# A seven-product down projection in another order: the bias row joins p1 on VectorE, and its second half reaches the residual by two transfers

## What is computed

```python
hc = conv_b + sum(conv_w[i] * hp[:, i:i + T] for i in range(CONV_WIDTH))
g, u = hc[..., :D_FF], hc[..., D_FF:]
y = jnp.einsum('btf,fd->btd', jax.nn.gelu(g, approximate=False) * u, w_down)   # D_FF = 2816, d = 1024
x = layer_norm(DEEPNORM_ALPHA * x + y, ln2_g, ln2_b)
```

## Time and profile before

| | us |
|---|---|
| time, median of 3 runs | 2312.85 (2310.52 to 2314.06) |
| the profiled execution | 2320.86 |
| its span, first to last instruction | 2319.1 |
| mean granted TensorE clock | 0.975 |
| PE busy | 2156.8 (93%) |
| DVE busy | 1605.3 (69%) |
| ACT busy | 1046.3 (45%) |
| POOL busy | 887.4 (38%) |
| down projection, first layer (first to last matmul on L2718) | from 883.9 |
| the same, second layer | to 2303.6 |
| DMA moved | 338.93 MB, mean 146 GB/s |

### The profile page before, as it was taken

One profiled execution on the slowest core, in us unless ns is written; L12 is line 12 of the kernel. 1 busy time (PEld: TensorE's weight loads), 2 busy tenths in 40 slices (PEclk: granted clock), 3 DMA queues, 4 the chain that ended last, 5 costly groups with the idle time before them and its releaser, 6 DMA issues.

```text
span 2319.1 us, 35307 instructions
## 1 busy us (share of the span) xinstructions
PE 2156.8 (93%) x13868; PEld 1937.6 (84%) x13868; DVE 1605.3 (69%) x2064; ACT 1046.3 (45%) x1867; POOL 887.4 (38%) x554
## 2 busy tenths in 40 slices
PE   7999999899999998789899999989999999988996
PEld 7997677899999997678688866769999999966775
DVE  1477767877777777455845687577777777775467
ACT  3226655444434444344522276464443444353543
POOL 1115255554455452121221342445545544333122
PEclk9999999999999999999999999999999999999998
DMA  5312166144554459999662112643455545699985
GB/s 156 84 33 67 34 203 181 61 121 124 141 147 121 132 130 296 257 250 226 162 163 54 48 49 94 171 147 90 113 144 141 129 125 142 165 277 266 251 194 158
DMA packets 258333, 338.93 MB, mean 146 GB/s; under 512 B 40048, under 2 KB 158576, under 8 KB 258096
## 3 DMA queue, kind: packets, MB, share of 16 engines
q1 hardware_dynamic: 223288, 261.70, 35.7%
q0 software_dynamic: 34880, 74.98, 19.0%
HBM read 217.65 MB, written 98.03 MB: 136 GB/s over the span
## 4 chain that ended last, share of the span: by engine, by line
PE 67%; DVE 14%; DMA 7%; ACT 5%; issue 4%; POOL 3%; SPq 0%; ACTq 0%; DVEq 0%; POOLq 0%
PE ps L2626 36%; PE ps L2718 10%; PE ps L2306 10%; PE ps L2565 5%; DMA araw<-a_scr 4%; DMA w<-in_w_down 2%; DVE dl L1914 2%; DVE al L1918 1%; PE ps L2449 1%; PE ps L2369 1%; PE ps L2475 1%; DVE bnst L1665 1%; DVE rzc L1652 1%; PE ps L2464 1%; PE ps L2428 1%
## 5 line engine op out<-in xcount | busy, mean ns | idle before, releaser
L2626 PE MATMUL ps<-bt,bh 128*128 128x272 f32 (+1 forms) x3520 | 591.4, 290 | 18.8 <-DVE bt L1823 9.4
L2626 PEld LDWEIGHTS ps<-bt,bh 128*128 128x128 f32 x3520 | 503.5, 190 | 20.4 <-DVE bt L1823 9.8
L1278 ACT ACTIVATE bh<-wblk 128x512 fp32r<-128x512 f32 x308 | 183.1, 623 | 490.8 <-POOL wblk L979 290.8
L2626 PE MATMUL ps<-bt,bl 128*128 128x272 f32 (+1 forms) x1760 | 369.4, 290 | 0.0
L2718 PE MATMUL ps<-dh,ah 128*128 128x512 f32 x616 | 251.6, 408 | 53.9 <-DVE al L1918 40.8
L2626 PEld LDWEIGHTS ps<-bt,bl 128*128 128x128 f32 x1760 | 278.5, 190 | 0.0
L967 POOL TENSOR_TENSOR bl<-wblk,bh 128x512 fp32r<-128x512 f32 x98 | 160.7, 1641 | 295.2 <-ACT bh L1278 295.2
L1841 DVE TENSOR_TENSOR bl<-wblk,bh 128x512 fp32r<-128x512 f32 x210 | 162.2, 805 | 140.0 <-ACT bh L1278 140.0
L2718 PE MATMUL ps<-dl,ah 128*128 128x512 f32 x616 | 247.3, 401 | 0.0
L2718 PE MATMUL ps<-dh,al 128*128 128x512 f32 x616 | 246.5, 400 | 0.0
L1914 DVE TENSOR_TENSOR dl<-w,dh 128x512 fp32r<-128x512 f32 x154 | 142.8, 928 | 140.7 <-ACT dh L1368 140.4
(11 more groups left out here) (260 smaller groups left out, 4322.4 us busy)
## 6 DMA issues: line engine op xcount, KB each, us to landing
wblk<-in_w_up SPq DMA_DIRECT2D x88, 512.0 KB, 5.9
a_scr<-hg SPq DMA_DIRECT2D x44, 552.0 KB, 3.5
e_scr<-hg POOLq DMA_DIRECT2D x44, 512.0 KB, 5.7
araw<-a_scr SPq DMA_DIRECT2D x66, 256.0 KB, 4.8
w<-in_w_down SPq DMA_DIRECT2D x66, 256.0 KB, 10.1
araw<-e_scr SPq DMA_DIRECT2D x66, 256.0 KB, 6.5
w<-in_w_down POOLq DMA_DIRECT2D x16, 1024.0 KB, 17.2
wrow<-in_w_out SPq DMA_DIRECT2D x48, 256.0 KB, 4.9
```

Source lines behind the costliest of these rows:

```text
L1278: act.activation(bh[b][:], block_of(f, b), ACT.Copy).then_inc(S["u_hi"], 1)
L2626: e = nc.tensor.matmul(up_half(f, b, n), lhs, rhs[:, c:HW_] if n else rhs[:, 0:c], start=(k == 0 and m == 0), stop=(k == HK - 1 and m == 2))
```

## The change

The order of the products becomes P1, P2, P3, P5, P6, P7, P4, and what is joined where changes with it:

- DVE takes P1 out of PSUM and adds the bias row's half 0 on the way (first_out, slots 10 and 11, 4 times 128 x 512), so p1 carries it. row_step (slot 12) turns the bias row's half 1 into the difference of its halves. first_join (slots 16 to 19) adds p1 to the top's half 0.
- Transfers: R_P1T adds p1 to the top's half 1, R_DT and R_DB add the difference to half 1 of the top and of the bottom, and R_U3B and R_U3C add U3 to both halves of the bottom, 1 MB each. R_8, R_TOP, R_P1, R_BOT and the three of U2 are gone. POOL adds the bias row to tile 8 by an addition.
- P5 is joined in slots 44 to 47 (VT, VB), P6 is joined to the top in slot 55, U2 = p1 + P6 goes into a tile of its own, un, in slots 56 and 61, and U3 = U2 + P7 in slot 66. There are no joins C22 and P7. C21 waits for R_U3C, the statistics of the bottom's half 1 (slots 71 and 73) for R_U3B.
- POOL's list: the residual's tiles stand one by one between other transfers; R_U3B and R_U3C come behind the five gained of TOP.
- Layer norm of TOP: DVE computes (x - mean) * gain[2] (spread, slots 58 to 62, 128 x 1024), ACT multiplies by 1/deviation (normal2, slots 60 to 64), and POOL has only the transfer of gain[3].
- SP issues the two transfers of first_gains one activation block earlier.

```diff
-P_1, P_2, P_3, P_6, P_5, P_7, P_4 = range(NP)
+P_1, P_2, P_3, P_5, P_6, P_7, P_4 = range(NP)
...
-P_BANKS = {P_1: PX, P_2: PY, P_3: PX, P_6: PY, P_5: PX, P_7: PY, P_4: PZ}
-P_SAMP = {P_1: PY[3], P_2: PX[0], P_3: PY[0], P_5: PY[0]}
+P_BANKS = {P_1: PX, P_2: PY, P_3: PX, P_5: PY, P_6: PX, P_7: PY, P_4: PZ}
+P_SAMP = {P_1: PY[3], P_2: PX[0], P_3: PY[0], P_5: PX[0]}
...
+        un = at("un", [P, 4, T], x_off)[:, :, HT:2 * HT]
...
                 first_blocks(l, 2, 4, 7)
+                first_gains(l)
                 act_block(l, 4)
                 first_blocks(l, 3, 7, KP)
-                first_gains(l)
...
                 pool.tensor_tensor(rz, rz, gain[0][0:q, :], ALU.mult).then_inc(S["xp"], 1)
+                if t == NB:
+                    pool.wait_ge(S["xp"], xp_n(l, NB))
+                    pool.tensor_tensor(rz, rz, gain[1][0:q, :], ALU.add).then_inc(S["xp"], 1)
...
+                if which == R_P1T:
+                    pool.wait_ge(S["p1_ev"], P1_EV * l + 4)
+                    pool.wait_ge(S["xp"], xp_n(l, 3) + 1)
+                    out, src = rz_top[:, :, HT:D], p1[:]
+                elif which in (R_DT, R_DB):
+                    pool.wait_ge(S["p1_ev"], P1_EV * l + 5)
+                    pool.wait_ge(S["xp"], xp_n(l, 3 if which == R_DT else 7) + 1)
+                    out = rz_top if which == R_DT else rz_bot
+                    out, src = out[:, :, HT:D], gain[1][:, HT:D].unsqueeze(1).to_broadcast([P, 4, HT])
+                else:
+                    pool.wait_ge(S["joins"], JOINS * l + J_U3 + 4)
+                    out, src = rz_bot[:, :, HT:D] if which == R_U3B else rz_bot[:, :, 0:HT], un
                 pool.dma_start(out, src, accum_op=ALU.add).then_inc(S["radd"], 16)
...
                 residual(l, NB)
-                residual_add(l, R_8)
                 act_add(l, KP - 2, 2)
                 act_add(l, KP - 1, 0)
-                for t in range(4):
-                    residual(l, t)
+                residual(l, 0)
                 act_add(l, KP - 1, 1)
-                residual_add(l, R_TOP)
+                residual(l, 1)
                 weight_add(l, T_1, 0)
+                residual(l, 2)
                 act_add(l, KP - 1, 2)
-                residual_add(l, R_P1)
+                residual(l, 3)
                 weight_add(l, T_1, 1)
+                residual_add(l, R_P1T)
                 weight_add(l, T_1, 2)
-                for t in range(4, NB):
-                    residual(l, t)
-                residual_add(l, R_BOT)
-                for which in (T_2, T_3, T_4):
-                    for g in range(len(KGRP)):
-                        weight_add(l, which, g)
-                for which in (R_U2T, R_U2B, R_U2C):
-                    residual_add(l, which)
+                residual_add(l, R_DT)
+                for g in range(len(KGRP)):
+                    weight_add(l, T_2, g)
+                    residual(l, 4 + g)
+                weight_add(l, T_3, 0)
+                residual(l, 7)
+                weight_add(l, T_3, 1)
+                residual_add(l, R_DB)
+                weight_add(l, T_3, 2)
+                for g in range(len(KGRP)):
+                    weight_add(l, T_4, g)
                 for t in TOP:
                     gained(l, t)
+                residual_add(l, R_U3B)
+                residual_add(l, R_U3C)
...
+            def first_out(l, i):
+
+                dve.wait_ge(S["d_tile"], 4 * (l * NP + P_1) + i + 1)
+                dve.tensor_tensor(p1[:, i, :], ps[:, PX[i], :], gain[1][:, 0:HT], ALU.add).then_inc(S["p1_ev"], 1)
+
+            def row_step(l):
+
+                dve.tensor_tensor(gain[1][:, HT:D], gain[1][:, HT:D], gain[1][:, 0:HT], ALU.subtract).then_inc(S["p1_ev"], 1)
+
+            def first_join(l, i):
+
+                dve.wait_ge(S["p1_ev"], P1_EV * l + i + 1)
+                dve.wait_ge(S["xp"], xp_n(l, i) + 1)
+                rz = half_of(i, 0)
+                dve.tensor_tensor(rz, rz, p1[:, i, :], ALU.add).then_inc(S["joins"], 1)
...
+            def spread(l, t):
+
+                q = tokens(t)
+                rz = rzd[t][0:q, :]
+                dve.wait_ge(S["ln_ag"], ln2_n(l, t) + 1)
+                dve.wait_ge(S["gain_landed"], 64 * (l + 1))
+                dve.scalar_tensor_tensor(out=rz, in0=rz, scalar=mv2[0:q, t, 0:1], in1=gain[2][0:q, :], op0=ALU.subtract, op1=ALU.mult)\
+                    .then_inc(S["ln_nm"], 1)
...
+                    elif 44 <= s < 48:
+                        for i in range(2):
+                            join(l, J_VT if s < 46 else J_VB, 2 * (s % 2) + i)
+                    elif s == 55:
                         for i in range(4):
-                            second(l, i)
...
+                            join(l, J_P6, i)
+                    elif s == 56:
+                        second(l, 0)
+                        second(l, 1)
+                    elif s == 57:
+                        for t in range(2):
+                            stats(l, t, 1)
+                            moments2(l, t)
+                    elif 58 <= s < 64:
+                        if s >= 59:
+                            scaled2(l, TOP[s - 59])
+                        if s < 63:
+                            spread(l, TOP[s - 58])
+                        if s < 61:
+                            stats(l, TOP[s - 56], 1)
+                            moments2(l, TOP[s - 56])
                         if s == 61:
-                            scaled2(l, NB)
-                    elif s == 65:
-                        for i in range(4):
-                            join(l, J_C22, i)
+                            second(l, 2)
+                            second(l, 3)
                     elif s == 66:
                         for i in range(4):
-                            join(l, J_P7, i)
-                    elif s in (67, 69):
+                            third(l, i)
+                    elif s in (71, 73):
```

More of the change, by code:

```diff
@@ L1400, in normal2 @@
                 act.wait_ge(S["ln_nm"], z2_n(l, t) + 1)
-                act.activation(rzd[t][0:q, :], rzd[t][0:q, :], ACT.Identity, scale=rst2[0:q, t, :], bias=nmr2[0:q, t, :]).then_inc(S["ln_z"], 1)
+                act.wait_ge(S["ln_rs"], ln2_n(l, t) + 1)
+                bias = zero2[0:q, 0:1] if t in TOP else nmr2[0:q, t, :]
+                act.activation(rzd[t][0:q, :], rzd[t][0:q, :], ACT.Identity, scale=rst2[0:q, t, :], bias=bias).then_inc(S["ln_z"], 1)
             def body(l):
@@ L2229, in body @@
                         sample_part(l, 0, 0, P_SAMP[P_1])
+                        first_out(l, 0)
+                        first_out(l, 1)
+                    elif s == 11:
+                        first_out(l, 2)
+                        first_out(l, 3)
+                    elif s == 12:
+                        row_step(l)
+                    elif 16 <= s < 20:
+                        first_join(l, s - 16)
                     elif s == 21:
```

110 lines of the change are left out of this document (38 added, 72 removed).

## The result

The changed kernel takes 2287.45 us (median of four runs, 2284.95 to 2291.31) where the kernel before takes 2313.20 in the same session: ratio 0.9892, 95% interval 0.9875 to 0.9909. That is 25.8 us gained, where the prediction said 52. The profiled execution takes 2286.33 us; the two profiled spans, 2319.1 and 2284.6, differ by 34.5, since the one of before lies 8 us over its median (2320.86 against 2313.20) and this one 1 us under.

What follows compares the result with a forecast made beforehand. TensorE holds 67% of the chain of waits, so its stops in the down projection were taken to bound time. Gains 16.2+8.6+15.1+14.9-3 = 51.8, near 52, off the median 2312.85 give 2261 us; range 2240 to 2290.

Steps and rivals of the forecast that it cites:

- main forecast: The whole run with every term as forecast: 2261 us, 2250 to 2272 by the bounds; chance 0.51.
- rivals 1 and 2 together: DMA engines keep the step 19 or 20 stop whole, and held VectorE time only moves: 2289 us.
- rival 1: DMA engines' load decides B: B stays whole (+8.6), steps 26 to 36 lose 5; 2275 us, chance 0.15.
- B: TensorE stop at step 19 or 20, ScalarE waiting for an activation block; gain 8.6 us, bounds 0 and 24.6.
- A: TensorE stop at step 10, VectorE held by POOL's residual products; cutting them up gains 16.2 us.
- the end: End of the down stage: U3 transfers land late behind five gain transfers; cost 3 us, bounds 0 and 9.
- C: TensorE stop at the start of the fourth product, waiting for T2; gain 15.1 us, bound below 10.
- D: TensorE stops in steps 60 to 65, POOL's gain multiplications holding dl; gain 14.9 us, bounds 8 and 17.
- Rival 2: Held VectorE time only moves: half of A (+8) and of D (+6) stay; 2275 us, chance 0.12.
- Step 1: Transfers onto the residual: 5 MB in for 8.25 out; before the fourth product, 5 MB become 2.
- Rival 4: Software queue doesn't serve in order, R_DB lands late and the VB join waits; slower, 2324 us, chance 0.06.
- Rival 3: B vanishes too, the software queue's 7 us earlier work sufficing; 2245 us, with no tail 2242; chance 0.13.

Runs made afterwards that it cites:

- e_bot_late: Kernel before, with the 2 MB bias transfer to rz_bot issued behind T2's three parts instead of ahead; ratio 0.9981 to the kernel before.
- e_all: Changed kernel, residual products of tiles 0 to 8 on VectorE, last layer's U3 earlier, SP's small transfers later, residual tiles 4 to 7 fetched later; 2251.71 us, ratio 0.9725.
- e_own_waits_light: e_own_waits with last layer's U3 earlier, SP's small transfers at steps 44 to 49, residual tiles 4 to 7 at steps 28 to 34; ratio 0.9827.
- e_one_run: Changed kernel with POOL's products of tiles 0 to 3 in one go again, not one between two transfers each; ratio 0.9896 to the kernel before.
- e_one_run_waits: e_one_run with POOL waiting for its own previous product before each residual product of tiles 0 to 7; ratio 0.9885 to the kernel before.
- e_own_waits: Changed kernel with POOL waiting for its own previous product before each residual product of tiles 0 to 7; ratio 0.9851 to the kernel before.

## Why the prediction was right and wrong

The direction was right, the size wasn't: 25.8 us came of the 52. 2287 lies inside the range, but outside the band of the main forecast and of rivals 1 to 3 taken singly. That it is near rivals 1 and 2 together (2289) is luck, since rival 1 had B stay whole and B fell to less than half. By the table the sum misses 20.8 us in A, 8.1 at the end and 2.5 in C, and gets back 8.0 in B and 4.1 in D. Of TensorE's lost time in the down stage, about a third was to be left; two thirds are (61.7 of 95.5 us).

- **A failed, at the sentence "A dl or al is held for at most one 2.6 us piece (10.42/4)".** It took for granted that the joint between two of POOL's instructions lets VectorE go because something else is issued there. Shown: 7.37 and 14.23 us holds over joints with issues alone, and A falling to 5.6 by waits alone. 20.8 us of the sum (16.2 forecast, 4.6 lost). The lines were there: in the earlier trace rows one dl was held for 11.71 us over four products, four instructions and three joints, while around 986 to 994 us of the same trace (not in the rows) VectorE came free behind single products, after holds of 2.67, 2.92 and 1.70 us: how two products follow each other mattered, and it wasn't asked. "Tile 8's extra POOL addition (2.4 us) holds VectorE where it is about 3 us ahead" failed by the same step: it is where the 7.37 begins, and it took 2.87. Rival 2 named the mechanism with "half of A (+8)"; all of it was left.
- **C held** (12.6 for 15.1), and e_bot_late shows its cause. What is missing is the 1.4 us stop at the turn: POOL's product of tile 5, now issued there, holds a dl (3.72 us at 1003.40); e_all shows it.
- **B was right in its mechanism and under-sized** (16.6 for 8.6). "While the software queue is backlogged, each step falls 1.7 us behind" is what the runs show in kind, at 4.2 us a step (e_own_waits_light) and not 4.9. Its second cause, SP's pause, which the prediction let keep half of B, decides nothing alone.
- **D was near in size (19.0 for 14.9, over the bound of 17) and mostly wrong in cause**: putting POOL's products back costs 3.8 / 3.6; the rest went with the slots' other work, of which no part was tried alone.
- **The end failed in size**, at "with part of the 256 KB ahead of it and its own 9.0": 13.7 us to landing in the last layer and 13.3 in the first, in company with the 256 KB and the stores of y. The wait on VectorE was 8.68 us, not 3, and TensorE lost 7.5 us by it in the second layer, against 2 to 3. The first layer's 4.0 instead of 0.5 is half POOL's late wl, a wait that the prediction doesn't have. Together they are 11 us, over the bound of 9.
- **Step 1's arithmetic and the serial issue of the five (23.5 for 23.8 us) held. Rival 4 didn't come**: R_DB, issued at 1030.69, was there when the join wanted it at 1053.60, no wait. The Trainium skill says that within one queue of one DMA engine descriptors start in order ("DMA: Bandwidth & Descriptors", section "Two DMAs through the same engine are not ordered"). This fits it. Rival 3, B gone, took two more moves on top of the products' and the tail's.
- The rule cited from the Trainium skill ("SBUF — State Buffer", section "Who interferes with whom") has whoever issues first keep the shared port pair for the whole instruction. The runs agree that products of POOL hold a two-operand piece of VectorE (2.39 us for the piece at 910.29), and that the pieces with one operand in PSUM aren't held (about 0.65 each beside POOL's run in the earlier trace rows), but the hold lasted over several instructions of POOL. Read as one instruction, the rule would give a single product's 2.9 to 3.4 us at most; the measurement, 14.23, decides.

## What to carry to other kernels

Where two engines share something and one holds the other, look in the trace for what ended each long hold, before counting on a cut: here a wait of POOL for its own result did, an issue of a transfer didn't, and moving the work to the engine that was held was best of all (25 us). A stage whose loads are limited by the DMA engines can take back time that was saved ahead of it, as B did in the kernels with waits, so see what is queued there first. And a transfer put at the end of a serial list should be costed with everything that runs beside it, not at its solo time.

## What was not expected of the hardware

- A dl or al that was held by POOL ended 0.54 to 0.56 us behind the end of a POOL product, in the changed kernel and e_one_run that of the last product of the stretch, over gaps of up to 1.3 us with issues in them. Held ones had begun inside a product or up to 0.84 us before one shows, but beginning near a product's start doesn't always mean being held (912.61: 0.68 us). A POOL issue alone didn't hold: a dl at 1040.00 beside one took 0.69 us.
- A wait of POOL for its own last product let VectorE go wherever it stood, though it hardly shows: as a gap of 0.07 us (910.21 + 2.39, then 912.67), of 0.14 in e_one_run_waits, and as nothing new in the 1.3 us behind the addition in e_own_waits. The wait costs POOL little: the four products of tiles 0 to 3 in one go took 11.67 us with it and 10.02 without.
- Beside 2.86 MB of the software queue the hardware queue moved 2.94 MB in 22 us, and beside 2.31 MB it moved 3.96: 0.55 MB less on the one stood beside 1.0 MB more on the other. These are two kernels whose loads differ, so what the one queue costs the other isn't shown by it.
